# Sparse attention's compression: first weights in the stream of chunks, split operands, every second column

## The reference, cut to what matters

```
q, kc, vc, ks, vs, kw, vw, gate, z = jnp.split(u @ w_in, points, axis=-1)
def compress(kv, pe, w1, w2):              # kv [1, 512, 4 groups, 64]
    nc = (s - CMP_BLOCK) // CMP_STRIDE + 1             # 31 blocks of 32 positions, 16 apart
    idx = jnp.arange(nc)[:, None] * CMP_STRIDE + jnp.arange(CMP_BLOCK)[None, :]
    blocks = kv[:, idx] + pe[None, None, :, None, :]
    flat = jnp.moveaxis(blocks, 3, 2).reshape(b, nc, g, CMP_BLOCK * dh)
    return jax.nn.silu(flat @ w1) @ w2                 # w1 [2048, 128], w2 [128, 64]
```

## Time and profile before

| | |
|---|---|
| median of 3 runs | 2083.43 us (2083.24 to 2084.54) |
| the profiled execution's own time | 2085.87 us |
| its span, first to last instruction | 2084.6 us |
| PE busy | 2044.4 us, 98% |
| DVE / ACT / POOL busy | 964.6 / 780.6 / 324.9 us |

### The profile page before, as it was taken

The page is one execution under the profiler, slowest core; times in us unless marked ns, Lnnn a source line. Parts: engine busy times, 40 slices in busy tenths (PEclk is TensorE's granted clock), DMA queues, the critical chain, the costliest instruction groups (busy, mean ns, idle before and its releaser), DMA issues.

```text
span 2084.6 us, 26714 instructions
## 1 busy us (share of the span) xinstructions
PE 2044.4 (98%) x10149; PEld 1658.4 (80%) x10149; DVE 964.6 (46%) x1968; ACT 780.6 (37%) x1552; POOL 324.9 (16%) x497
## 2 busy tenths in 40 slices
PE   7999999999999999999999999999998999999998
PEld 5887888888888886788888888888787888777766
DVE  4438434443354344435534443364435664535455
ACT  4226332222232223333322222243336884435453
POOL 2103100000002120000110000041003764312211
PEclk9999999999999999999999999999998999999999
DMA  5330243333324331132243333225321103323212
GB/s 178 102 98 14 61 134 91 95 98 94 99 79 137 99 97 46 51 101 93 68 135 100 95 97 100 93 84 160 117 78 55 32 22 102 114 74 109 67 46 81
DMA packets 96766, 187.32 MB, mean 90 GB/s; under 512 B 8407, under 2 KB 16639, under 8 KB 96512
## 3 DMA queue, kind: packets, MB, share of 16 engines
q1 hardware_dynamic: 90288, 164.35, 26.1%
q0 software_dynamic: 6352, 21.27, 3.2%
HBM read 181.33 MB, written 4.26 MB: 89 GB/s over the span
## 4 chain that ended last, share of the span: by engine, by line
PE 91%; ACT 5%; DVE 2%; issue 1%; POOL 1%; DMA 0%; SPq 0%; ACTq 0%; DVEq 0%; POOLq 0%
PE bank L750 62%; PE bank L786 10%; PE bank L1261 5%; PE bank L1020 2%; PE bank L1182 1%; PE bank L1159 1%; PE bank L824 1%; PE bank L1275 1%; ACT sc L1804 1%; PE bank L849 1%; PE bank L1005 1%; PE bank L1091 1%; PE bank L1298 1%; ACT xn L1798 1%; PE bank L1148 1%
## 5 line engine op out<-in xcount | busy, mean ns | idle before, releaser
L1975 DVE TENSOR_TENSOR wl<-raw,wh 128x1024 fp32r<-128x1024 f32 x306 | 375.8, 1232 | 774.3 <-ACT wh L1378 773.4
L1378 ACT ACTIVATE wh<-raw 128x1024 fp32r<-128x1024 f32 x306 | 321.0, 1053 | 827.3 <-PE bank L750 785.3
L750 PE MATMUL bank<-hTh,wh 128*128 128x512 f32 (+2 forms) x1200 | 467.5, 390 | 0.2 <-issue 0.2
L750 PE MATMUL bank<-hTl,wh 128*128 128x512 f32 (+2 forms) x1200 | 466.9, 389 | 0.0
L750 PE MATMUL bank<-hTh,wl 128*128 128x512 f32 (+2 forms) x1200 | 466.9, 389 | 0.0
L750 PEld LDWEIGHTS bank<-hTh,wh 128*128 128x128 f32 (+2 forms) x1200 | 223.9, 187 | 48.5 <-issue 0.3
L750 PEld LDWEIGHTS bank<-hTh,wl 128*128 128x128 f32 (+2 forms) x1200 | 223.9, 187 | 48.4
L750 PEld LDWEIGHTS bank<-hTl,wh 128*128 128x128 f32 (+2 forms) x1200 | 223.9, 187 | 47.9
L750 PE MATMUL bank<-wh,hTh 128*128 128x512 f32 x400 | 156.5, 391 | 0.1
L750 PE MATMUL bank<-wh,hTl 128*128 128x512 f32 x400 | 155.7, 389 | 0.0
L750 PE MATMUL bank<-wl,hTh 128*128 128x512 f32 x400 | 155.6, 389 | 0.0
(11 more groups left out here) (383 smaller groups left out, 3111.9 us busy)
## 6 DMA issues: line engine op xcount, KB each, us to landing
raw<-in_ffn_w_in SPq DMA_DIRECT2D x88, 512.0 KB, 3.7
raw<-in_ret_w_in SPq DMA_DIRECT2D x48, 512.0 KB, 3.8
raw<-in_ffn_w_out SPq DMA_DIRECT2D x44, 512.0 KB, 3.7
raw<-in_diff_w_in SPq DMA_DIRECT2D x32, 512.0 KB, 3.8
raw<-in_fox_w_in SPq DMA_DIRECT2D x24, 512.0 KB, 4.0
raw<-in_nsa_w_in SPq DMA_DIRECT2D x20, 512.0 KB, 3.7
raw<-in_ret_w_out SPq DMA_DIRECT2D x16, 512.0 KB, 3.7
raw<-in_fox_w_out SPq DMA_DIRECT2D x8, 512.0 KB, 3.6
```

Of the source, the lines that this page charges most:

```text
L750: i = pe.do.matmul(dst, x, y, start=first and k == 0 and q == 0, stop=stop)
L1378: act.do.activation(M.hl[n % HL_SLOTS][0][:, 0:m], M.raw[n % RAW_SLOTS][:, 0:m], ACT.Copy).then_inc(*T.up("act_hi", n))
L1975: dve.do.tensor_tensor(wl[:, 0:m], M.raw[n % RAW_SLOTS][:, 0:m], wh[:, 0:m].bitcast(F32), ALU.subtract).then_inc(*T.up("dve_lo", n))
```

## The change

The first weights w1 of keys and values become 2 chunks each of the stream, behind `nsa sw` and behind `nsa z0`; they are loaded by SP and split by ACT and DVE as all others. `kvc` is replaced by a high half `kvh` and a low half `kvl` in float32r, of 256 columns a group: column m holds position 2m in partitions 0 to 63 and position 2m + 1 in partitions 64 to 127. The step between blocks is so 8 columns. Each hidden(w) is 48 matmuls of 160 columns (32 a group, the last of each unused). The take of `nsa c` now reads every second column of a bank; where the half of the partitions changes, ACT writes a copy to `xn` (`moved_c`) first, and both halves are made from it.

```
--- before.py
+++ after.py
+    chunks.extend(("w1k", r0, 8, ((0, 128),)) for r0 in (0, 1024))
     chunks.append(("nsa", 0, 8, ((2560, 48),)))
     block8("nsa", (2608, 512))
+    chunks.extend(("w1v", r0, 8, ((0, 128),)) for r0 in (0, 1024))
     block8("nsa", (3120, 512))
-                a.kvc = [sb(sub, "kvc", [128, 5, S]) for _ in range(2)]
+                a.kvf = [[sb(sub, name, [128, 1288], F32R) for name in ("kvh", "kvl")] for _ in range(2)]
@@ pool_nsa
-    load_w1("k")
-    pool.wait_ge(*at("pe_cmp", ("hidden", 0)))
-    load_w1("v")
@@ pe_nsa, hidden(w)
-        for t in range(16):
-            i = pe.do.matmul(M.bank[b][:, 0:155].rearrange("p (g c) -> p g c", g=5),
-                             M.xn[t // 8][:, t % 8 * 128:t % 8 * 128 + 128], a.kvc[w][:, :, 2 * t:2 * t + 481:16],
-                             start=t == 0, stop=t == 15)
+        for c in range(2):
+            pe_weights(pe, T, n)
+            for k in range(nk):
+                t = c * nk + k
+                h, l = (bass.AP(tensor=x.tensor, offset=t, ap=[[1288, 128], [256, 5], [8, 32]]) for x in (y[:, :] for y in a.kvf[w]))
+                for q, (x, y) in enumerate([(wh, h), (wh, l), (wl, h)]):
+                    i = pe.do.matmul(out, x[:, k, :], y, start=t == 0 and q == 0, stop=t == 15 and q == 2)
@@ act_nsa, take_c(o)
-            act.do.activation(a.kvc[o // 2][0:64, 2 * (o % 2) + g2, :], M.bank[bank["nsa c"][o]][64 * g2:64 * g2 + 64, :], ACT.Copy).then_inc(
-                *up("act_kvc", o))
+            for r in range(2):
+                h = a.kvc[o // 2][0][64 * r:64 * r + 64, 2 * (o % 2) + g2, :]
+                src = M.bank[bank["nsa c"][o]][64 * g2:64 * g2 + 64, r:512:2]
+                if r != g2:
+                    moved = moved_c(M, o, r)
+                    act.do.activation(moved, src, ACT.Copy).then_inc(*up("act_kvc", ("moved", o, g2)))
+                    act.wait_ge(*at("act_kvc", ("moved", o, g2)))
+                    src = moved
+                act.do.activation(h, src, ACT.Copy).then_inc(*up("act_kvc", o))
@@ act_nsa, dve_nsa
-    hidden(1)
+    act_product(act, T, M, 2, 1, lambda o: hidden(1))
-    pev(1)
+    dve_product(dve, T, M, 2, 1, lambda o: pev(1))
@@ dve_nsa, take_c(o)
-            src = M.bank[bank["nsa c"][o]][64 * g2:64 * g2 + 64, 1:512]
-            dve.do.tensor_copy(a.kvc[o // 2][64:128, 2 * (o % 2) + g2, 0:511], src).then_inc(*up("dve_kvc", o))
+            for r in range(2):
+                h, l = (x[64 * r:64 * r + 64, 2 * (o % 2) + g2, :] for x in a.kvc[o // 2])
+                src = M.bank[bank["nsa c"][o]][64 * g2:64 * g2 + 64, r:512:2] if r == g2 else moved_c(M, o, r)
+                dve.do.tensor_tensor(l, src, h.bitcast(F32), ALU.subtract).then_inc(*up("dve_kvc", o))
```

More of the change, by code:

```diff
@@ L237, in memory @@
         "fox": I["fox_w_in"][0], "foxo": I["fox_w_out"][0], "ret": I["ret_w_in"][0], "reto": I["ret_w_out"][0],
+        "w1k": I["nsa_cmp_w1_k_2"][0], "w1v": I["nsa_cmp_w1_v_2"][0],
         "ffi0": I["ffn_w_in"][0], "ffi1": I["ffn_w_in"][1], "ffo0": I["ffn_w_out"][0], "ffo1": I["ffn_w_out"][1],
@@ L318, in memory @@
             with ExitStack() as sub:
-                a.kvc = [sb(sub, "kvc", [128, 5, S]) for _ in range(2)]
+                a.kvf = [[sb(sub, name, [128, 1288], F32R) for name in ("kvh", "kvl")] for _ in range(2)]
+                a.kvc = [[x[:, 0:1280].rearrange("p (g m) -> p g m", g=5) for x in xs] for xs in a.kvf]
+                a.pem = sb(sub, "pem", [128, 2, 16])
                 a.w2, a.pev = sb(sub, "w2", [128, 2, 128]), sb(sub, "pev", [128, 2])
@@ L361, in query, with moved_c @@
     return M.nsa.Q0[:, h, :] if h < 8 else (M.HTh if h < 12 else M.HTl)[:, h % 4, :]
+def moved_c(M, o, r):
+    return M.xn[o // 2][64 * r:64 * r + 64, o % 2 * 512 + r * 256:o % 2 * 512 + r * 256 + 256]
 def attended(M, t):
@@ L591, in load_bt @@
         pool.do.dma_start(a.BT[h % 4][:, :], src).then_inc(*up(f"bt{h % 4}", h, step=16))
[L593 to L597, removed]
     for w in range(2):
[L600 to L603, removed]
+        for x in a.kvf[w]:
+            pool.do.memset(x[:, 1024:1288].bitcast(F32), 0.0).then_inc(*up("pool_pad", (w, 1)))
     for w, n in enumerate("kv"):
@@ L608, in pool_nsa @@
     pool.do.memset(a.vcmp[:, :, :, :], 0.0).then_inc(*up("pool_pad", "values"))
-    pool.wait_ge(*at("pe_turned", ("n4", 2, 1)))
-    pool.wait_ge(*at("pe_turned", ("n4", 3, 1)))
-    load_w1("k")
-    pool.wait_ge(*at("pe_cmp", ("hidden", 0)))
-    load_w1("v")
+    pool.wait_ge(*at("pe_product", ("nsa hidden", 0)))
     for h in range(4):
@@ L1083, in hidden @@
         pe_bank(pe, T, b)
-        pe.wait_ge(*at(f"ldw1{'kv'[w]}", "w1"))
         pe.wait_ge(*at("dve_pe", 1))
@@ L1089, in hidden @@
         pe.wait_ge(*at("pool_pad", (1, 1)))
-        for t in range(16):
-            i = pe.do.matmul(M.bank[b][:, 0:155].rearrange("p (g c) -> p g c", g=5),
-                             M.xn[t // 8][:, t % 8 * 128:t % 8 * 128 + 128], a.kvc[w][:, :, 2 * t:2 * t + 481:16],
-                             start=t == 0, stop=t == 15)
-        i.then_inc(*up("pe_cmp", ("hidden", w)))
+        out = M.bank[b][:, 0:160].rearrange("p (g c) -> p g c", g=5)
+        for c in range(2):
+            n = pe.use
+            pe.use += 1
+            wh, wl, nk = chunk_views(M, n)
+            pe_weights(pe, T, n)
[4 more added lines that the diff above has]
+                    i = pe.do.matmul(out, x[:, k, :], y, start=t == 0 and q == 0, stop=t == 15 and q == 2)
+            i.then_inc(*up("pe_product", ("chunk", n), *[("nsa hidden", w)] * (c == 1)))
         pe.free[b] = [("act_hid", w)]
@@ L1731, in take_c @@
         for g2 in range(2):
-            act.do.activation(a.kvc[o // 2][0:64, 2 * (o % 2) + g2, :], M.bank[bank["nsa c"][o]][64 * g2:64 * g2 + 64, :], ACT.Copy).then_inc(
-                *up("act_kvc", o))
+            for r in range(2):
[3 more added lines that the diff above has]
+                    moved = moved_c(M, o, r)
+                    for t in range(4):
+                        act.wait_ge(*at("pe_turned", ("n4", t, 1)))
+                    act.do.activation(moved, src, ACT.Copy).then_inc(*up("act_kvc", ("moved", o, g2)))
+                    act.wait_ge(*at("act_kvc", ("moved", o, g2)))
+                    src = moved
+                act.do.activation(h, src, ACT.Copy).then_inc(*up("act_kvc", o))
     def take_sw(o):
@@ L1757, in hidden @@
     def hidden(w):
-        act.wait_ge(*at("pe_cmp", ("hidden", w)))
+        act.wait_ge(*at("pe_product", ("nsa hidden", w)))
         act.wait_ge(*at("dve_pev", w))
-        act.do.activation(a.hid[:, w, :], M.bank[bank["nsa hidden", w]][:, 0:124], ACT.Silu, bias=a.pev[:, w:w + 1]).then_inc(*up("act_hid", w))
+        act.do.activation(a.hid[:, w, :].rearrange("p (g c) -> p g c", g=4),
+                          M.bank[bank["nsa hidden", w]][:, 0:128].rearrange("p (g c) -> p g c", g=4)[:, :, 0:31], ACT.Silu, bias=a.pev[:, w:w + 1]).then_inc(*up("act_hid", w))
     def take_q(base):
@@ L1767, in take @@
             act.wait_ge(*at("pe_product", (f"nsa q{base}", o)))
-            act.wait_ge(*at("pe_cmp", ("hidden", 1)))
+            act.wait_ge(*at("pe_product", ("nsa hidden", 1)))
             if t >= 2:
@@ L1780, in act_nsa @@
     act_product(act, T, M, 4, 4, take_sw)
-    hidden(0)
+    act_product(act, T, M, 2, 1, lambda o: hidden(0))
     act_product(act, T, M, 1, 1, take_gate)
     act_product(act, T, M, 4, 4, take_z(0))
-    hidden(1)
+    act_product(act, T, M, 2, 1, lambda o: hidden(1))
     act.wait_ge(*at("pe_cmp", "keys"))
@@ L2480, in pev @@
     def pev(w):
-        dve.wait_ge(*at("pe_cmp", ("hidden", w)))
-        dve.do.tensor_copy(a.pev[:, w:w + 1], M.bank[bank["nsa hidden", w]][:, 124:125]).then_inc(*up("dve_pev", w))
+        dve.wait_ge(*at("pe_product", ("nsa hidden", w)))
+        dve.do.tensor_copy(a.pev[:, w:w + 1], M.bank[bank["nsa hidden", w]][:, 128:129]).then_inc(*up("dve_pev", w))
     def take_q(base):
@@ L2503, in dve_nsa @@
     for w in range(2):
-        src = M.bank[bank["nsa positions"]][0:64, w * 32:w * 32 + 32]
-        dve.do.tensor_copy(a.kvc[w][0:64, 4, 0:32], src).then_inc(*up("dve_pe", w))
-        dve.do.tensor_copy(a.kvc[w][64:128, 4, 0:31], src[:, 1:32]).then_inc(*up("dve_pe", w))
+        for r in range(2):
+            src = M.bank[bank["nsa positions"]][0:64, w * 32 + r:w * 32 + 32:2]
+            h, l = (x[64 * r:64 * r + 64, 4, 0:16] for x in a.kvc[w])
+            if r:
+                dve.do.tensor_copy(a.pem[64:128, w, :], src).then_inc(*up("dve_pe", ("moved", w)))
+                dve.wait_ge(*at("dve_pe", ("moved", w)))
+                src = a.pem[64:128, w, :]
+            dve.do.tensor_copy(h, src).then_inc(*up("dve_pe", ("high", w, r)))
+            dve.wait_ge(*at("dve_pe", ("high", w, r)))
+            dve.do.tensor_tensor(l, src, h.bitcast(F32), ALU.subtract).then_inc(*up("dve_pe", w))
     dve_product(dve, T, M, 4, 4, take_sw)
-    pev(0)
```

(3 more changed lines are left out.)

## The result

The changed kernel takes 2088.95 us (median of 14 runs, 2087.16 to 2089.63); the kernel before, run beside it on the same chip, takes 2084.18 (14 runs, 2083.05 to 2086.03). The ratio is 1.0023, 95% interval 1.0015 to 1.0030: slower by 4.8 us, 3 to 6 by the interval. The direction was forecast; the size was not (+15.4). Every execution behind the numbers of this document had a mean granted clock of 0.99 or more; one of run 5 (2911.03 us at 0.66) had not and is left out.

The account below looks back on a forecast made before the run. PE was taken to bound the kernel (91% of the chain), so only its longer work or waits count. 9.2 + 4.0 + 2.15 = 15.4 us takes the median from 2083.43 to 2098.8 us; range 2086 to 2102.

Parts of the forecast that it names:

- Step 1: Matmuls of hidden(w): 48 strided float32r ones at 0.271 us, 13.0 us each time; +4.6 us each, +9.2 for both.
- rival A: Hidden(w)'s price goes by passes: 0.149 us a matmul, 7.2 us for 48; sum +3.7, 2087.1 us; chance 0.26.
- Step 2: Take of `nsa c`: ACT needs 2.6 us an output, so PE waits in `nsa sw`'s first chunk; +4.0 us, bounds +0.8 and +7.4.
- rival C: Take of `nsa c`: ACT's copies overlap, and hidden(w) gets cheaper as a rival has it; 2082.2 to 2083.9 us; chance 0.04.
- Step 3: Four more splits on ACT and DVE: hidden except behind hidden(1), where they delay `nsa z4`; +2.15 us.
- Steps 4 to 6: w1 loads by SP, DVE's small position operations, POOL's memsets and its wait for hidden(0): all cost nothing.
- PEclk 1.00: Expected sign in the changed kernel's trace: PE's granted clock stays at 1.00.
- rival D: Clock falls in PE's waits, on top of the forecast: a few us of half speed, about 2103 us; chance 0.05.

Follow-up runs that it names:

- run 5: Changed kernel with the takes behind hidden(1) put ahead of the next chunk's split, and POOL making ACT's two `xn` copies: 2081.21 us, ratio 0.9989 to the kernel before.
- Run 1: Measuring version of the changed kernel: hidden(0) in float32r, hidden(1) in float32 read 480 columns at eight steps; only start distances count, 0.404 us at 32 bytes in float32r.
- run 4: Changed kernel with POOL making the two copies from `xn` to `kvh` for each output of `nsa c`, DVE subtracting those parts last: 2085.48 us, ratio 1.0007 to before.
- Run 6: Changed kernel with hidden(0) and hidden(1) reading 32 neighbouring columns of each row, not every 8th: 2087.54 us, ratio 1.0018 to the kernel before.
- run 3: Changed kernel with the takes behind hidden(1) moved ahead of the next chunk's split on ACT and DVE: 2083.26 us, ratio 1.0002 to the kernel before.

## Why the prediction was right or wrong

**Step 1 failed, and with it the size.** "I take the strided row as the nearest, and its 1.70 ns as the time in which one column that stands alone is fetched, whatever is then done with it": that gave 0.271 us a matmul, 13.0 us and +9.2 for both. Measured: 0.138 us, 6.63 us, -3.6 for both. Run 1 shows what was wrong: the price of a lone column goes with the type, 0.85 ns in float32r and 1.7 in a float32 record, and not with the step. This was rival A, with 0.149 us and 7.2 us; its price is shown, its reason (a fetch for each pass) is not. The row taken as the nearest differed from the new matmul in two things, the step and the type, and the text ascribed its factor of two to the one and carried it over to the other. The rows held the hint on which rival A was built: float32 has half of float32r's pace when contiguous too. The fixed part of 166 ns in the text's 0.83 ns is 175 by its own rows, which makes 0.81 and changes nothing.

**Step 2 held.** +4.0 forecast, +3.7 measured; 2.6 us an output forecast, 2.51 measured; the waits are at the outputs named, three of the four for `kvl`. Neither bound (ACT overlapping its copies, reading every second column slower) was met. With the first of them rival C fell too.

**Step 3 held in size, not in its last steps.** +2.15 forecast for the splits, +1.8 measured at full clock (run 4), +2.25 with the 0.4 of the clock. The text had PE wait for `kcml` and wrote "Keys and values fit into that". The wait is for the copy of the gates, and values stood on the path between it and `nsa z4`. No wait to speak of at `nsa z0`: right, but barely, with hidden(0) at 6.6 us; Silu ended at 1479.72 and `nsa z0` began at 1479.77. Run 6 shows the wait at 5.3.

**Steps 4 to 6 held** (loads, positions, POOL at nothing): no wait for any of them is in the list of waits.

**"PEclk 1.00" was wrong,** and rival D came in small, and not on top of the forecast but of rival A: 2.0 us at the level of 1.2 GHz. The text had the row of a longer gap at 0.59 and of a shorter one at 1.00 and left it a chance of 0.05.

**The sum.** Rival A as it stood was +3.7. With the measured terms it is 3.7 + 1.8 - 3.6 = +1.9, and the clock puts 2.0 on top: +3.9, for 4.3 in the stage and 4.8 by the medians. A together with D had no chance of its own in the text. That the direction came out rests on the take, the tail and the clock; the largest term, step 1, had the wrong sign. That the range held the time was luck: its lower end reached into A. The chances did not fit, with 0.58 on a forecast whose largest term came from one row and one assumption.

## What to carry to other kernels

Where a cost is read from a row that differs from the new operation in two things at once, work the sum by either explanation before choosing, and give each the chance that the rows give it; here a factor of two in type and in step looked alike. A take that grows is paid where the next product writes its banks, and a split that moves into a queue ahead of a short chain of small operations is paid in full, and here once more in the clock (1.8 us and 2.0): put such a chain ahead of the long operation. When a product is made shorter, ask what will be waited for at its end: the gain of hidden(0) was lost at the next bank.

## What the runs showed of the hardware that was not expected

- A float32r matmul takes 0.22 us for 480 columns if they come in fours of neighbours, and 0.40 to 0.43 if they come singly (8, 12, 16, 24, 32, 64 bytes apart) or in pairs; 0.59 at 48 bytes. A float32 record takes 0.40 to 0.43 for fours, pairs, or every second column, 0.64 for every third and 0.80 to 0.86 beyond.
- A float32r matmul of 160 columns that stand side by side in rows of 32 starts every 0.111 us (run 6), hardly below the 0.12 of one of 256.
- The same tail gave different slow stretches. With the gap the granted clock was 0.5 for 6.83 us from 0.8 us behind the start of pev (the changed kernel), for 3.41 us from 4.1 us behind it (run 4), and for 3.41 from 3.85 behind it (run 6, 1512.67); without it 1.00 (runs 3 and 5). The slow stretch at the start of the attention, which all kernels here have, lasted 17.07 us in the profiled execution before, 13.65 in those of the changed kernel and of runs 4, 5 and 6, and 10.24 in that of run 3. The time from the end of the stage to the end of the program goes with it: 511.6 us, 510.4 to 510.5 (all four), and 508.7, though nothing was changed there. So up to 3 us between two profiled executions lie in this stretch and not in the stage that was edited. What sets its length was not tried, nor how it falls in the other runs.
